# Spreading the choice of experts over more columns, and placing a pass's steps by room on three engines

## The reference, cut to what matters

```python
x = x + w_out(sigmoid(g_A) * (o_A @ w_o_a) + sigmoid(g_B) * (o_B @ w_o_b))
def fn(t):                                   # the experts, for a row t = RMSNorm(x)
    q = (t @ wq).reshape(blk, 8, 128)
    s1 = einsum('thd,hnd->thn', q[..., :64], subkeys[:, 0])
    s2 = einsum('thd,hnd->thn', q[..., 64:], subkeys[:, 1])
    v1, i1 = top_k(s1, 16); v2, i2 = top_k(s2, 16)
    sc, pos = top_k((v1[..., :, None] + v2[..., None, :]).reshape(..., 256), 16)
    e = i1[pos // 16] * 128 + i2[pos % 16]   # 128 experts of 16384 for each row
    a = gelu(einsum('td,thkd->thk', t, u[e]))
    return einsum('thk,thkd->td', softmax(sc) * a, v[e])
```

## Time and profile before

| | |
|---|---|
| median of three runs | 1808.41 us (1806.15 to 1809.05) |
| the profiled execution | 1809.06 us, its span 1807.2 us |
| DVE busy | 1310.1 us, 72% |
| PE busy | 1254.0 us, 69%, mean granted clock 0.77 |
| POOL busy | 527.0 us, 29% |
| DMA | 696.47 MB, mean 385 GB/s |
| gathers alone | 570.53 MB in 544 gathers |

### The profile page before, as it was taken

The page is one execution under the profiler, slowest core; times in us unless marked ns, Lnnn a source line. Parts: engine busy times, 40 slices in busy tenths (PEclk is TensorE's granted clock), DMA queues, the critical chain, the costliest instruction groups (busy, mean ns, idle before and its releaser), DMA issues.

```text
span 1807.2 us, 26391 instructions
## 1 busy us (share of the span) xinstructions
PE 1254.0 (69%) x9056; PEld 696.8 (39%) x9056; DVE 1310.1 (72%) x3857; ACT 579.8 (32%) x1995; POOL 527.0 (29%) x569
## 2 busy tenths in 40 slices
PE   8989877678877575788876576679877544434343
PEld 3677532445545232454534233446545111111111
DVE  5563796889666667898766668999666768686754
ACT  2231133333423333333333234343333222222222
POOL 0100232233322322333322323333322433333332
PEclk9989888688898596877899597887998555555555
DMA  6237799999999999999999999999999999999997
GB/s 266 78 95 292 282 414 422 363 425 424 402 423 423 424 423 418 375 396 403 425 423 421 425 422 383 425 389 401 420 423 420 414 427 426 425 427 426 426 416 305
DMA packets 119380, 696.47 MB, mean 385 GB/s; under 512 B 17983, under 2 KB 21118, under 8 KB 49102
## 3 DMA queue, kind: packets, MB, share of 16 engines
q0 software_dynamic: 78848, 570.53, 75.8%
q1 hardware_dynamic: 36686, 121.83, 17.4%
q10 hardware_dynamic: 3712, 2.43, 0.4%
HBM read 691.65 MB, written 3.02 MB: 384 GB/s over the span
## 4 chain that ended last, share of the span: by engine, by line
DMA 31%; DVE 28%; PE 25%; issue 7%; ACT 4%; POOL 1%; ACTq 1%; DVEq 0%; POOLq 0%
DMA rows<-in_peer_uv,index 22%; DVE rows L2646 11%; PE ps_v L1814 6%; PE ps_f L1553 4%; DMA wch<-in_w_row 3%; PE ps_f L1568 3%; DMA wch<-in_w_out 3%; PE ps_h L1794 2%; PE ps_f L1347 2%; DVE score L2322 2%; DMA wch<-in_w_uq 1%; DVE best L2321 1%; PE ps_f L1431 1%; PE ps_f L1471 1%; ACT diag L2158 1%
## 5 line engine op out<-in xcount | busy, mean ns | idle before, releaser
L1324 POOL DMA_INDIRECT rows<-in_peer_uv,index x544 | 517.2, 951 | 1183.1 <-PE ps_v L1814 1004.3
L2646 DVE CUSTOM_DVE_ANT_0 rows<-rows,ps_h 128x1024 f32<-128x1024 f32 x544 | 656.4, 1220 | 269.7 <-DMA rows<-in_peer_uv,index 203.3
L1814 PE MATMUL ps_v<-rows,diag 128*32 128x256 f32 x4352 | 425.1, 507 | 428.0 <-ACT diag L2158 414.7
L1814 PEld LDWEIGHTS ps_v<-rows,diag 128*32 128x32 f32 x4352 | 125.5, 131 | 680.6 <-ACT diag L2158 549.8
L2149 ACT ACTIVATE tan<-arg 128x2 f32<-128x2 f32 x272 | 55.4, 204 | 782.9 <-DVE arg L2656 704.7
L2152 ACT ACTIVATE weight<-tan,lead 128x1 f32<-128x1 f32 x544 | 180.8, 379 | 9.2
L2158 ACT ACTIVATE diag<-sel,weight 128x32 f32<-128x32 f32 x544 | 140.9, 306 | 0.4 <-PE ps_v L1814 0.3
L1553 PEld LDWEIGHTS ps_f<-bufh,wch 128*128 128x128 f32 x768 | 113.6, 232 | 21.2 <-issue 19.0
L1553 PE MATMUL ps_f<-bufh,wch 128*128 128x128 f32 x768 | 119.6, 320 | 0.0
L1347 PE MATMUL ps_f<-wch,bufh 128*128 128x512 f32 (+1 forms) x192 | 84.6, 583 | 22.9 <-DMA wch<-in_w_row 20.7
L1347 PEld LDWEIGHTS ps_f<-wch,bufh 128*128 128x128 f32 x192 | 34.2, 209 | 68.5 <-issue 37.6
(11 more groups left out here) (398 smaller groups left out, 1685.5 us busy)
## 6 DMA issues: line engine op xcount, KB each, us to landing
wch<-in_w_gate SPq DMA_DIRECT2D x60, 512.0 KB
wch<-in_w_row SPq DMA_DIRECT2D x36, 512.0 KB
wch<-in_w_o SPq DMA_DIRECT2D x32, 512.0 KB
wch<-in_w_out SPq DMA_DIRECT2D x24, 512.0 KB
wch<-in_peer_wq SPq DMA_DIRECT2D x24, 512.0 KB
rows<-in_peer_uv,index POOLq DMA_INDIRECT x544
w_tok<-in_w_tok SPq DMA_DIRECT2D x4, 1640.0 KB, 13.7
wch<-in_w_uq SPq DMA_DIRECT2D x6, 384.0 KB
```

Source lines behind the costliest of these rows:

```text
L1324: pool.indirect_dma_start(rows[c % RING][:, :, :].rearrange("p a d -> p (a d)"), None, io.peer_uv[:, :], at).then_inc(s_uv[c % RING], 16)
L1814: ins = nc.tensor.matmul(ps_v[GROUP * a:GROUP * (a + 1), :], diag[:, c % DRING, :], rows[c % RING][:, 1, QD * a:QD * (a + 1)], start=False ...
L2646: v.tensor_tensor_reduce(out=u, in0=u, in1=ps_h[:, :], scale=1.0, scalar=0.0, op0=ALU.mult, op1=ALU.add, accum_out=dots[:, c % KEEP:c % KE ...
```

## The change

Two tables of places change; no instruction is added, removed or altered.

- `AHEAD`: for a block that is not the first of its tile the 11 parts of the choice stand at columns -7, -4, -1, 2, 5, 8, 11, 14, 17, 19 and 22 counted from the first column of the block before. The first block of a tile keeps 2, 4, ..., 22, since its scores come last in a pass, and block 1 keeps 11 to 21.
- `spread_steps`: each column now has room for steps on PE, DVE and ACT apart (2.0, 1.6 and 2.3 us), less where a part of the choice (1.5 on DVE), a spread (0.5 on PE), a block's store (2.1 on ACT) or its successor (0.6 on PE) stands. A step starts where the fullest engine has room for it. All costs are scaled by one factor so that the steps fill the pass.

```diff
@@ -708,6 +708,7 @@
 NP = len(PASSES)
 CHUNKS = 3 * DC + DC + PH + 1
 PARTS = 11
+AHEAD = (-7, -4, -1, 2, 5, 8, 11, 14, 17, 19, 22)
 NSUMS = 3 + NPAIR + 3 * H
 S_Q = 3 + H + 1
 S_R = S_Q + H
@@ -750,16 +751,37 @@
         self.base = START if p else 0
 
 
+def choice_columns():
+
+    at = {}
+    for n in range(1, NB):
+        first = SG * (n - 1)
+        for j in range(PARTS):
+            if n == 1:
+                k = CHOICE_AT + j
+            elif BLOCKS[n][1] > 0:
+                k = AHEAD[j]
+            else:
+                k = 2 * (j + 1)
+            at[first + k] = (n, j)
+    return at
+
+
+CHOICES = choice_columns()
+
+
 def step_work(p):
 
     at, nk, chunks = Ticks(p), META + P * (p + 1), p + 1
-    small, wide = 0.28, 0.89
+    small, wide, table = 0.28, 0.89, 1.3
     row = 0.16 + nk / 960
+    shape = 0.18 + nk / 1240
     piece = 2 * (nk / 2400 * 2 + 0.05)
-    pe_head = {5: DC * small, 8: 7 * small, 13: 3 * small, 16: 4 * 0.67 + 2 * wide, 23: 9 * small, 26: 2 * H * small}
+    pe_head = {5: DC * small, 13: 3 * small, 16: 4 * 0.67 + 2 * wide, 23: 9 * small, 26: 2 * H * small}
     pe_head.update({x: 4 * wide for x in range(7, 13) if x != 8})
     pe_head.update({8: 7 * small + 4 * wide, 13: 3 * small + DC * small})
     dve_head = {2: 1.5, 4: 1.3, 6: 1.4, 10: 1.3, 12: 1.0, 16: 1.8, 18: 2.1, 19: 2.0, 21: 1.9, 22: 3.0, 23: 1.8, 24: 2.0, 25: 1.5}
+    act_head = {3: table, 9: 0.6, 10: 1.1, 11: 0.6 + table, 13: 0.6, 14: 1.0, 17: 2.7, 20: table, 24: 1.5, 27: 2.4}
 
     def unit_at(k, lag):
         w, r = divmod(k - lag, U)
@@ -768,7 +790,9 @@
     work = []
     for k in range(-at.base, at.all):
         x = k + START - SETTLE
-        pe, dve = (pe_head.get(x, 0), dve_head.get(x, 1.5 if x < 2 and p > 1 else 0)) if k < 0 else (0, 0)
+        pe, dve, act = (head.get(x, 0) if k < 0 else 0 for head in (pe_head, dve_head, act_head))
+        if k < 0 and x < 2:
+            dve = 1.5 if p > 1 else 0
         if unit_at(k, 0) is not None:
             pe += piece
         if (unit_at(k, 3) or 0) >= H:
@@ -777,6 +801,14 @@
             pe += chunks * small
         if 0 <= k < 6 * DC and k % 6 in (2, 4):
             pe += DC * small
+        if 0 <= k < 6 * DC and k % 6 == 5:
+            act += 0.4
+        if (u := unit_at(k, 1)) is not None and u < H:
+            act += shape
+        if (unit_at(k, 2) or 0) >= H:
+            act += shape + 0.3
+        if (unit_at(k, 4) or 0) >= H:
+            act += shape + 0.2
         if (u := unit_at(k, 2)) is not None and u < H:
             dve += row
         if (u := unit_at(k, 1)) is not None and u >= H:
@@ -785,27 +817,71 @@
             dve += 0.9
         if k in (at.turn, at.rows, at.res) or at.mix <= k < at.mix + DC or at.ask <= k < at.ask + PH:
             pe += DC * small
+        if k in (at.turn + 1, at.rows + 1):
+            act += 1.2
         if at.mix + 1 <= k < at.mix + 1 + DC:
             dve += 0.7
         if at.out <= k < at.out + 4:
             pe += 4 * wide
+            act += 1.0
         if k == at.res:
             dve += 2.7
+            act += table
         if k == at.res + 1:
             dve += 1.5
+        if at.ask + 1 <= k < at.ask + 1 + PH:
+            act += 0.3
         if k in (at.key, at.key + 1):
             pe += 1.3
-        work.append((pe, dve))
+        if k in (at.key + 1, at.key + 2):
+            act += 1.2
+        work.append((pe, dve, act))
     return work
 
 
+def rooms(p):
+
+    left = []
+    for k in range(SLOTS):
+        pe, dve, act = 2.0, 1.6, 2.3
+        if SLOTS * (p - 1) + k in CHOICES:
+            dve -= 1.5
+        if k % SG == SG - 1:
+            pe -= 0.5
+        if k >= SG and k % SG == LAG - 1:
+            act -= 2.1
+        if k >= SG and k % SG == LAG:
+            pe -= 0.6
+        left.append((pe, dve, act))
+    return left
+
+
 def spread_steps(p):
 
     first_col, last_col = 0 if p > 1 else AFTER_TILE, SLOTS - 4
-    ends = list(itertools.accumulate(pe + dve + 0.3 for pe, dve in step_work(p)))
-    share = lambda k: (min(max(k, first_col), last_col) - first_col + 0.001) / (last_col - first_col)
-    done = [sum(e <= ends[-1] * share(k) for e in ends) for k in range(SLOTS + 1)]
-    return [done[k + 1] - done[k] for k in range(SLOTS)]
+    work, left = step_work(p), rooms(p)
+    sums = [[0.0] + list(itertools.accumulate(room[e] for room in left[first_col:])) for e in range(3)]
+
+    def after(e, t, us):
+        c = min(int(t), SLOTS - first_col - 1)
+        have = sums[e][c] + (t - c) * left[first_col + c][e] + us
+        while c + 1 < SLOTS - first_col and sums[e][c + 1] < have:
+            c += 1
+        return c + (have - sums[e][c]) / left[first_col + c][e]
+
+    def ends(scale):
+        t, at = 0.0, []
+        for step in work:
+            t = max(after(e, t, scale * us) for e, us in enumerate(step)) + 0.1 * scale
+            at.append(t)
+        return at
+
+    low, high = 0.1, 20.0
+    for _ in range(50):
+        scale = (low + high) / 2
+        low, high = (scale, high) if ends(scale)[-1] <= last_col - first_col else (low, scale)
+    at = [0.0] + ends(low)[:-1]
+    return [sum(c <= first_col + t < c + 1 for t in at) for c in range(SLOTS)]
 
 
 STEPS = {}
@@ -2683,10 +2759,8 @@
                         dot(b)
                     if b >= 2:
                         next(second, None)
-                    if n == 0 and 0 <= k - CHOICE_AT < PARTS:
-                        choose(1, k - CHOICE_AT)
-                    if 0 < n < NB - 1 and k % 2 == 0 and 1 <= k // 2 <= PARTS:
-                        choose(n + 1, k // 2 - 1)
+                    if b in CHOICES:
+                        choose(*CHOICES[b])
 
 
 class Names:

```

## The result

The changed kernel took 1855.81 us (median of 4 runs, 1852.61 to 1856.93); the kernel before, run on the same chip beside it, 1808.73. The ratio is 1.0255, with an interval of 1.0231 to 1.0280: 46 us slower by the ratio (47 by the medians), where 1796.5 had been predicted.

What follows compares the result with a forecast made beforehand. Transfers were taken to bound the kernel. Terms of -10.4 and -1.5 us, the others 0, summed to -11.9 from 1809.06, giving 1797.2, or 1796.5 as median; range 1786 to 1814, the likeliest case alone 1787 to 1805.

Steps and rivals of the forecast that it cites:

- Joins: Where head and units join in the fronts: losses between 0 and 10.7 us, taken as 5, replace 15.4; -10.4 us.
- Selection and choice: Selection columns, now with parts of the choice: 4 us lost in place of 5.5; -1.5 us.
- DVE's worst stretch: Front 3, columns 50 to 73: DVE's excess over the transfers' need is 8.7 us, before 3.2; 5.5 us worse.
- entered with a cushion that the join didn't take: Front 3's selection begins with 10 us of lateness that transfers survive still unspent, so only 3.6 us is lost.
- Head: First steps of a front: start at the same column, end six or seven later; 0 us, from -1 to +2.
- Tail: Last steps of a front: 24 chunks go from 31 columns to 26 or 27, covered by transfers; 0 us, up to +3.
- The rest: Small dips elsewhere, 9.5 us, left as they are; 0 us, from -5 to +4.
- index steps in their relu's column: Slower rival, fronts 1 to 3: 17 waits of 5.1 us each, 37.9 us lost in place of 15.4; 1830 us, chance 0.16.
- PE's clock: Slower rival, tail: pauses lower the clock to 0.65, 10 us lost a pass; 1826 us, chance 0.05.
- dips at columns 55 to 80 in all three passes: Sign in the new profile, passes with fronts 1 to 3: such dips would show the forecast wrong; no size given.

Runs made afterwards that it cites:

- joins-only kernel: Kernel before, fronts 2 and 3 only: turn of the heads one column earlier, their copies and first unit one or two later; 1807.46 us, ratio 0.9973.
- light gates: One of eight products per gate made in fronts 1 to 3: changed kernel 1874.19 us, ratio 1.0375; kernel before 1811.21 us, ratio 1.0007.

## Why the prediction was wrong

Its frame held: transfers bound the kernel, and the loss can be read as GB/s under 426. Its sum of terms did not. Two steps failed: the head put at nothing, and the selection priced by DVE's work alone.

- **Joins**, -10.4: right in sign, mis-sized. The holes now found there are 364 to 376 us at 299 GB/s, 731 to 734 at 189, 1145 to 1148 at 202 and 1172 to 1178 at 272, by the same formula 3.6, 1.7, 1.6 and 2.2 us, and 1.4 more at 708 to 716 at 353: 10.5 for 15.4, so -5 us. The joins-only kernel won 5 as well, but nearly all in front 2.
- **Selection and choice**, -1.5: this is a step that failed, by about 19 us: the selection units cost 18. The prediction counted DVE's work and had it right: for front 3 it forecast 69.6 us in columns 47 to 70 before and 75.1 in 50 to 73 now, and the traces have DVE busy for 67.7 and 74.1. It never asked when PE would deliver the scores. "DVE's worst stretch" was treated as one engine with a load; it is two engines handing work to each other, and in columns 48 to 80 of front 3 11.8 us of waits came on top. In front 2, where it forecast no loss, the stretch grew by 5.6 us with no more work, at scores that stand in their logits' column. Nor was it "entered with a cushion that the join didn't take": the stretch grew by work and waits in full.
- **Head**, 0 (-1 to +2): the other step that failed, by 20 us by the ratios (9 to 11 in the traces), in front 1. The argument was DVE's 2.4 us per column. The chunks of weights were counted in the need of the transfers, but not that PE waits for them and makes the projections in the columns right before the spread at column 32, which is queued behind the last: DVE waited 14.0 us there.
- **Tail**, 0 up to +3: right, 3 us (0 to 7 by the interval), although DVE's waits for the residual, L2496, grew from 3.8 us to 27.9. With the new tail alone they are 27.4 us as well, at the ratio 1.0018, so the transfers made them good.
- **The rest**, 0: units 16 to 23 were not looked at by themselves. Their scores went from 15 to 18 columns into 11 to 14 and cost some 7 us; the holes from 873 to 889 and 1304 to 1323 us are theirs, the first with one wait of 6.5 us for scores in whose column the logits stand as well.

Of the rivals, *index steps in their relu's column* gave the sign and nearly the first half of the size (1830), by the wrong mechanism: its waits came to 18 us, 15 of them, where 3.8 us a wait was needed. *PE's clock* was placed in the tail, and the mean clock did not fall at all (0.77 before and after); single products were slow after a wait, in the units and at the spread. The prediction named the sign that would refute it, "dips at columns 55 to 80 in all three passes". In front 3 that came; in front 2 there is one at columns 70 to 74 (844 to 854 us, 4.1 us) and the deepest stands at 80 to 83; in front 1 it is at 82. The rival's clock acts in the light gates, where it fell to 0.63 in front 3's stretch, but of the changed kernel's own loss no share of it is shown: that stretch stood at 0.79 before and 0.78 now.

What stays open: what four scores in their logits' column cost, apart from the others that stand one column ahead; the share of the indexer's units in the 18 us of head and indexer; why the new logits cost 6 us in front 3 at the old distance, though they lie within three columns of the old spacing shifted; and whether the 14.0 us wait or the wait for the latents' norm before it is what front 1 pays for.

## What to carry to other kernels

Before steps are moved, write for each stretch in which an engine is over 95% busy the list of products that it waits for, and how many columns ahead of the reader each is queued, with what stands before it in that queue; a load that adds up says nothing about the hand-over. What an edit costs in one order says little of another: scores one column ahead of the logits cost nothing in the kernel before (1.0007), and giving scores one column more won some 15 us in the changed one. When a reader and what it reads fall into one column, look at them one by one. And a hole that an order shows plainly is best mended by moving the two steps that make it, not all steps.

## What was not expected of the hardware

Leaving out seven eighths of the gates' products made the kernel slower, 1.0375 for 1.0255, with the granted clock at 0.714 for 0.77, while in the kernel before, at 0.722, it changed nothing. The spread, four products of 32 rows by 512 columns, took 1.92 us in one place and 3.71 in another; a sum that takes such a price from a row has to say at which clock the row stands.
